# Step columns and differential values in one product, the B by C products of both groups side by side, cumulated sums of both token halves at once

## What is computed

```python
for l in range(DEPTH):                       # DEPTH = 2
    h = rms_norm(x, attn_norm_w[l])
    proj = h @ w_in[l]
    a_q, a_k, a_v, b_z, b_xbc, b_dt, c_q, c_k, c_v = jnp.split(proj, offsets, axis=-1)
    y_a = windowed_gqa_sink(...)             # 6 heads, a_q, a_k, a_v
    y_b = ssd_mixer(b_z, b_xbc, b_dt, ...)   # Mamba-2, both directions, 2 state groups
    y_c = diff_attention(...)                # 4 heads, c_q, c_k, c_v
    x = x + jnp.concatenate([y_a, y_b, y_c], axis=-1) @ w_out[l]
    h = rms_norm(x, ffn_norm_w[l])
    x = x + hierarchical_moe(h, ...)
return rms_norm(x, final_norm_w)
```

## Time and profile before

| | us |
|---|---|
| three runs, median | 1211.71 |
| lowest, highest | 1211.57, 1214.07 |
| span of the profiled execution | 1213.5 |
| its own time, beyond the span | not listed apart |
| TensorE busy | 948.9 (78%) |
| VectorE busy | 398.7 (33%) |
| ScalarE busy | 189.6 (16%) |
| DMA engines, queue 1 | 86.5% of the span |

### The profile page before, as it was taken

One profiled execution on the slowest core, in us unless ns is written; L12 is line 12 of the kernel. 1 busy time (PEld: TensorE's weight loads), 2 busy tenths in 40 slices (PEclk: granted clock), 3 DMA queues, 4 the chain that ended last, 5 costly groups with the idle time before them and its releaser, 6 DMA issues.

```text
span 1213.5 us, 26544 instructions
## 1 busy us (share of the span) xinstructions
PE 948.9 (78%) x11004; PEld 600.0 (49%) x11004; DVE 398.7 (33%) x1231; ACT 189.6 (16%) x546; POOL 8.9 (1%) x27
## 2 busy tenths in 40 slices
PE   7999989766668787895799999895666666666964
PEld 6877855433334443453387777553333333333532
DVE  4778453111122222231176774431111111111213
ACT  2245221000001110110023352110000000000101
POOL 2000000000000000000000000000000000000000
PEclk9999989888789998997899999898888888787977
DMA  9835179999999999999995244899999999999994
GB/s 342 334 123 209 70 296 425 424 427 427 426 424 424 426 426 425 400 425 428 408 394 199 97 182 156 344 426 426 425 428 426 426 427 427 425 425 426 424 423 196
DMA packets 47435, 436.64 MB, mean 360 GB/s; under 512 B 8256, under 2 KB 10304, under 8 KB 21440
## 3 DMA queue, kind: packets, MB, share of 16 engines
q1 hardware_dynamic: 47296, 434.72, 86.5%
HBM read 433.65 MB, written 1.05 MB: 358 GB/s over the span
## 4 chain that ended last, share of the span: by engine, by line
PE 47%; DMA 37%; DVE 6%; issue 5%; SPq 2%; DVEq 2%; ACT 1%; another core or an unknown queue 1%; ACTq 0%
DMA ring<-in_w_up 37%; PE ps L601 13%; PE ps L689 8%; PE ps L617 5%; PE ps L812 4%; PE ps L626 3%; PE ps L569 3%; PE ps L701 2%; PE ps L589 2%; PE ps L706 1%; PE ps L752 1%; SPq L442 1%; SPq L440 1%; PE ps L791 1%
## 5 line engine op out<-in xcount | busy, mean ns | idle before, releaser
L601 PE MATMUL ps<-ring,xg 128*32 128x256 f32 x4352 | 317.3, 455 | 176.9 <-DMA ring<-in_w_up 171.5
L601 PEld LDWEIGHTS ps<-ring,xg 128*32 128x32 f32 x4352 | 170.0, 130 | 307.3 <-issue 247.1
L1135 DVE SCALAR_TENSOR_TENSOR th<-th,ps 128x128 f32<-128x128 f32 x72 | 20.7, 288 | 593.8 <-ACT th L934 593.8
L617 PE MATMUL ps<-ring,actT 128*32 128x256 f32 x2304 | 139.2, 382 | 13.5 <-issue 12.8
L617 PEld LDWEIGHTS ps<-ring,actT 128*32 128x32 f32 x2304 | 69.0, 109 | 74.6 <-DVE actT L1139 22.3
L934 ACT ACTIVATE th<-ps 128x128 f32<-128x128 f32 x72 | 20.0, 278 | 515.7 <-PE ps L601 480.1
L569 PE MATMUL ps<-xh,Pb 128*32 128x256 f32 x1152 | 79.4, 394 | 24.5 <-issue 20.4
L689 PE MATMUL ps<-hT,ring 128*128 128x256 f32 x416 | 95.3, 386 | 0.8 <-ACT hT L971 0.8
L689 PEld LDWEIGHTS ps<-hT,ring 128*128 128x128 f32 x416 | 78.6, 193 | 12.7 <-issue 1.4
L626 PE MATMUL ps<-ysb,PwT 32*128 32x256 f32 x992 | 71.8, 403 | 0.0
L569 PEld LDWEIGHTS ps<-xh,Pb 128*32 128x32 f32 x1152 | 38.5, 113 | 49.3 <-issue 24.5
(11 more groups left out here) (251 smaller groups left out, 744.0 us busy)
## 6 DMA issues: line engine op xcount, KB each, us to landing
ring<-in_w_down SPq DMA_DIRECT2D x62, 2048.0 KB, 40.4
ring<-in_w_gate SPq DMA_DIRECT2D x60, 2048.0 KB, 45.6
ring<-in_w_up SPq DMA_DIRECT2D x60, 2048.0 KB, 47.3
ring<-in_w_in SPq DMA_DIRECT2D x6, 2048.0 KB, 19.8
ring<-in_w_out SPq DMA_DIRECT2D x4, 2048.0 KB, 19.5
ring<-in_w_gate SPq DMA_DIRECT2D x8, 1024.0 KB, 29.1
ring<-in_w_up SPq DMA_DIRECT2D x8, 1024.0 KB, 31.8
ring<-in_w_in SPq DMA_DIRECT2D x4, 1024.0 KB, 21.3
```

The source lines that it names most:

```text
L601: last = mm(b_gate[j * SLOTS:(j + 1) * SLOTS, 0:2 * GQ], tokens[:, k, :], ring[:, low:high + 1:high - low, o:o + GQ], start=(k == 0), stop ...
L617: last = mm(b_y[j * SLOTS:(j + 1) * SLOTS, 0:DQ], actT[:, c * SLOTS:(c + 1) * SLOTS], ring[:, slot, o:o + DQ], start=(c == 0), stop=(c == ...
```

## The change

**The pieces of `w_in`.** The second piece held the last 128 columns of `xbc`, `dt` and `cq`; now it holds those 128, `dt` and `cv`, in two transfers. The fifth piece held `ck` and `cv`; now `cq` and `ck`. The widths stay 396 and 512.

**`dt` and `cv` in one product.** The TensorE steps `dt` and `cv` become `dc.0` and `dc.1`, one per token half, eight products of 268 columns each, at the place where `dt` was. ScalarE copies both into `dcv`, scaled; VectorE's `dt` step reads `dcv` and so waits for ScalarE.

**`cb` on TensorE** becomes one step `cB` where `cb.0` was: four products that alternate between the two 64-row halves, into two banks. ScalarE's `cb.g` copies stay where they were.

**`cum`**: three products over both token halves instead of six.

```diff
-W_IN_PIECES = [(O_XBC, 512), (O_XBC + 512, O_CK - O_XBC - 512), (O_AQ, O_AV), (O_AV, O_XBC - O_AV), (O_CK, D_IN - O_CK)]
+W_IN_PIECES = [[(O_XBC, 512)], [(O_XBC + 512, O_CQ - O_XBC - 512), (O_CV, D_IN - O_CV)], [(O_AQ, O_AV)], [(O_AV, O_XBC - O_AV)],
+               [(O_CQ, O_CV - O_CQ)]]
+DC = 2 * S_H + C_H * C_V
...
-    dt conv.4 ak silu.3 aq.0 dta xs.0 silu.4 sc.0 nm.0 aq.2 xs.1 aS.0 cum cumT aq.1 lam cb.0 sc.1 sc.2 seg.0.0
+    dc.0 dc.1 dt conv.4 ak silu.3 aq.0 dta xs.0 silu.4 sc.0 nm.0 aq.2 xs.1 aS.0 cum cumT aq.1 lam cB cb.0 sc.1 sc.2 seg.0.0
...
-    pT.2 cq.1 sc.5 pT.3 y.5 sc.6 cS.0 sc.7 oa.0 nm.5 ybn pT.4 nm.6 cv oa.1 pT.5 yT.0 yT.1 oa.2 sc.8 sc.9 sc.10
+    pT.2 cq.1 sc.5 pT.3 y.5 sc.6 cS.0 sc.7 oa.0 nm.5 ybn pT.4 nm.6 oa.1 pT.5 yT.0 yT.1 oa.2 sc.8 sc.9 sc.10
     nm.7 pT.6 cS.1 sc.11 sc.12 outA.0 pT.7 outA.1 od.0 nm.8 sc.13 nm.9 pT.8 od.1 outA.2 pT.9 od.2 od.3 outA.3 ycn
...
-    return {"xbc": int(step[-1] == 4), "dt": 1, "cq": 1, "aq": 2, "ak": 2, "vz": 3, "ck": 4, "cv": 4}.get(kind)
+    return {"xbc": int(step[-1] == 4), "dc": 1, "aq": 2, "ak": 2, "vz": 3, "cq": 4, "ck": 4}.get(kind)
...
+                    for c0, w in W_IN_PIECES[n][1:]:
+                        sp_.dma_start(to[:, :, IN_WIDTH[n] - w:], w_in[li, :, c0:c0 + w].rearrange("(k p) n -> p k n", p=P)
+                                      ).then_inc(signal, 16)
...
+                    elif kind == "dc":
                         w = piece(piece_of(s), s)
+                        t = s[1]
+                        for k in range(KC):
+                            last = mm(bank[:, 0:DC], hT[:, k, t * P:(t + 1) * P], w[:, k, P:P + DC], start=(k == 0), stop=(k == KC - 1))
...
+                        sums = bank[:, 0:TT * 4 * S_H].rearrange("p (t n) -> p t n", t=TT)
+                        mm(sums[:, :, 0:S_H], upto[:, :], dta[:, :, 0:S_H], start=True, stop=True)
+                        mm(sums[:, :, S_H:2 * S_H], since[:, :], dta[:, :, S_H:2 * S_H], start=True, stop=True)
+                        last = mm(sums[:, :, 2 * S_H:4 * S_H], ones[:, :], dta[:, :, 0:2 * S_H], start=True, stop=True)
...
+                        for t in range(TT):
+                            for g in range(S_G):
+                                r = slice(g * S_N, (g + 1) * S_N)
+                                last = mm(ps[BANK["cb", g]][:, t * SEQ:(t + 1) * SEQ], xc[r, 3, t * P:(t + 1) * P], xc[r, 4, :],
+                                          start=True, stop=True)
...
+                    elif kind == "dc":
                         act.wait_ge(done["dve"], nth(li, "dve", ("sq",)))
+                        last = A(dcv[:, s[1], :], bank[:, 0:DC], ACT.Copy, scale=root[:, TT + s[1]:TT + s[1] + 1])
...
+                        dve.wait_ge(done["act"], nth(li, "act", ("dc", 0), ("dc", 1)))
+                        v.tensor_tensor(z.rearrange("p (t n) -> p t n", t=TT), dcv[:, :, 0:n],
+                                        rowp[:, R_DTB:R_DTB + n].unsqueeze(1).broadcast_to([P, TT, n]), ALU.add)
```

More of the change, by code:

```diff
@@ L45 @@
 A_SCALE, C_SCALE = A_D ** -0.5, C_QK ** -0.5
-W_IN_PIECES = [(O_XBC, 512), (O_XBC + 512, O_CK - O_XBC - 512), (O_AQ, O_AV), (O_AV, O_XBC - O_AV), (O_CK, D_IN - O_CK)]
+W_IN_PIECES = [[(O_XBC, 512)], [(O_XBC + 512, O_CQ - O_XBC - 512), (O_CV, D_IN - O_CV)], [(O_AQ, O_AV)], [(O_AV, O_XBC - O_AV)],
+               [(O_CQ, O_CV - O_CQ)]]
+IN_WIDTH = [sum(w for _, w in piece) for piece in W_IN_PIECES]
+DC = 2 * S_H + C_H * C_V
 W_OUT_PIECES = [(0, 512), (512, 512)]
@@ L107 @@
 STEPS = [(name, *map(int, index)) for name, *index in (step.split(".") for step in ORDER.split())]
-ON_PE = {"xT", "rs", "xbc", "dt", "cq", "aq", "ak", "cum", "xs", "cb", "cumT", "rows", "aS", "cS", "y", "vz", "pT", "ck", "cv", "oa", "od",
+ON_PE = {"xT", "rs", "xbc", "dc", "cq", "aq", "ak", "cum", "xs", "cB", "cumT", "rows", "aS", "cS", "y", "vz", "pT", "ck", "oa", "od",
          "yT", "cT", "outA", "outB", "fT", "lg", "seed", "cnt", "rank", "ov"}
@@ L111 @@
           "lg", "route", "rank", "ov"}
-ON_ACT = {"sq", "rs", "par", "lam", "dta", "cumT", "silu", "row", "sc", "vz", "zs", "pT", "cv", "oa", "od", "yT", "cT",
+ON_ACT = {"sq", "rs", "par", "lam", "dta", "cumT", "silu", "row", "sc", "vz", "zs", "pT", "dc", "oa", "od", "yT", "cT",
           "xT", "xs", "cb", "sa", "xn2", "route"}
@@ L186, in reader @@
         return "act" if step[1] % 2 == 0 else "dve"
-    return "dve" if step[0] in ("xbc", "cq", "aq", "ak", "ck", "dt", "cum", "sc", "y", "lg", "cnt", "rank", "ov") else "act"
+    return "dve" if step[0] in ("xbc", "cq", "aq", "ak", "ck", "cum", "sc", "y", "lg", "cnt", "rank", "ov") else "act"
 PE_STEPS = list(COUNT["pe"])
@@ L203, in tenants @@
         return [("sc", A_H + 4 * step[1] + i) for i in range(4)]
+    if step[0] == "cB":
+        return [("cb", g) for g in range(S_G)]
     if step[0] == "rows":
@@ L701, in _ @@
                             last = mm(bank[:, :], hT[:, k, t * P:(t + 1) * P], w[:, k, :], start=(k == 0), stop=(k == KC - 1))
-                    elif kind == "cv":
-                        w = piece(piece_of(s), s)
-                        for t in range(TT):
-                            for k in range(KC):
-                                last = mm(bank[:, t * C_H * C_V:(t + 1) * C_H * C_V], hT[:, k, t * P:(t + 1) * P],
-                                          w[:, k, O_CV - O_CK:D_IN - O_CK], start=(k == 0), stop=(k == KC - 1))
                     elif kind == "cum":
@@ L992, in _ @@
                     elif kind == "cb":
+                        act.wait_ge(done["pe"], nth(li, "pe", ("cB",)))
                         last = A(CBs[s[1]][:, :, :].rearrange("p a b -> p (a b)"), bank[:, :], ACT.Copy)
```

46 lines of the change are left out of this document (13 added, 33 removed).

## The result

| | before | after |
|---|---|---|
| median of four runs, side by side | 1212.89 (1211.57 to 1215.15) | 1253.28 (1251.64 to 1254.08) |
| ratio, 95% interval | | 1.0329 (1.0309 to 1.0349) |
| span of the profiled execution | 1213.5 | 1250.8 (its own time 1252.65) |
| mixer of layer 0 (to the first gather of the experts) | 168.72 | 181.44 |
| experts of layer 0 | 438.18 | 446.67 |

The change made the kernel 3.3% slower. The stages are taken from the one profiled execution of each kernel and cut where TensorE's first gather (line 569, after the change 577) starts in each layer and where the last quarter of the experts' result is copied. The span grew by 37.3 us: 12.7 and 16.3 in the two mixers, 8.5 in the experts of layer 0.

A forecast was written before the change was run, and what follows sets the result against it. Experts wait for weights by DMA, the mixer for TensorE, with VectorE pacing its tail. Per layer 2.1 + 8.8 + 3.4 = 14.3 us, twice 28.6, on span 1213.5 gives 1242.1, less 1.8: 1240.3 us; range 1231 to 1252.

The forecast's parts named there:

- The sign: Whole kernel: slower, chance 0.93; faster 0.04, within 0.2% 0.03.
- Part 1: TensorE up to `cq.1`: `dc` +3.9, `cum` −0.7, `cB` −1.1, together +2.1 us per layer (bounds 2.0 to 3.3).
- `cB` paired: `cB` step: four products side by side cost 1.06 us, saving 1.06; if they did not pair, nothing.
- the rule of the Trainium skill weighed there: `dc`: weight loads overlap products only where row groups differ, giving 11.0 us; the forecast took 7.4 instead.
- Part 2: Tail without `cv`: VectorE's chain stays, TensorE idles from about 105.6 to 111.4; 7.17 us removed bring about 1.
- Part 3: Tail: `outA.0` waits for ScalarE's `pT.6` copy, +5.1 us; `outA.1` for VectorE's `sc.12` read, +8.8 per layer in all.
- Part 4: Both `outA` steps: the new waits lower the granted clock, 1.7 us each, +3.4 per layer.
- My reading of the earlier trace: `outB` before the change: two short waits around 143 us lowered the clock, 8.88 us for 7.17, 1.7 lost.
- 14.3 us in each layer: Each layer's mixer: 2.1 + 8.8 + 3.4 us, twice 28.6.
- their restart moves with the end of the mixer: Ring full before the experts: DMA bytes left stay the same, so every microsecond of a mixer's tail counts once per layer.
- the experts' stages as long as before: Experts of both layers: expected sign that the change leaves their length as it was.
- the median 1.8 us under the span: Whole kernel: median of runs 1211.71 against the profiled span 1213.5, so 1242.1 became 1240.3 us.

The follow-up runs named there:

- e1_banks: The changed kernel with PSUM banks renamed from `dc.0` to the first `outA` step, so neither `outA` step waits late for a bank; 1226.29 us, ratio 1.0105.
- e2_waits_alone: The kernel before with only bank numbers changed, so that `pT.6` lies in bank 0 and `sc.12` in bank 1; 1238.39 us, ratio 1.0202.
- the fourteen kernels: The kernels before and after the change and all follow-up kernels; experts of layer 1 took 433.7 to 437.3 us over them.
- the last four: The kernel before with 6, 12, 25 or 38 empty products per layer in the wait for the router's choice; 1218.00, 1221.52, 1236.60, 1239.79 us, one run each.
- e7_cum_cB: The kernel before with only the `cum` and `cB` edits, banks without late waits, no empty products added; 1214.20 us, ratio 1.0019.
- e9_shift38: The kernel before with 38 empty products of 4 columns per layer in the wait for the router's choice; 1239.79 us, one run.

## Why the prediction was wrong

The sign and most of the cause were right; the time was 13.0 us too low and 1.3 us above my range.

*Part 1, +2.1 up to `cq.1`:* `cqT` was copied at 98.65 against 96.92, +1.7: right in kind, 0.4 us too large. `dc` took 7.23 to 7.39 us (7.4 expected) and `cB` paired. By the rule of the Trainium skill weighed there (TensorE: Matmul & The Clock Gate, section Part 3: Packing small matmuls — row/col tiling) `dc` would have taken an estimated 11.0 us; the trace does not follow that rule, and the weight loads of these full-height products stayed hidden.

*Part 2, the lost cover:* a wait of 5.69 us for the gated norm where I had read off 5.8. Right; that the transposes, `oa.2` and `pT.6` behind it run at half speed (1.51 and 1.98 us for 0.84 and 1.09) was not in my sum. In the changed kernel it lies under `outA.0`'s wait; in e1_banks, with that wait gone, it stands on the path.

*Part 3, the banks:* `outA.0` at 123.14, expected 123.3; `outA.1` at 134.96, expected 134.7 with the clock's 1.7 in it. Shown from both sides by e1_banks and e2_waits_alone.

*Part 4, +3.4 for the clock:* the two steps lost 2.2 and 1.7 us in layer 0, 3.9 in all. In layer 1 they took 7.45 and 8.43 us, about 2.1 and 3.2 over full speed, 5.3 in all, so the term was too small there. On the other side `outB` of layer 0 took 7.2 us and not the 8.88 of the earlier trace rows, which gave 1.7 back; in layer 1 it took 8.86. My reading of the earlier trace rows, that two short waits had cost that clock, does not stand: the same two waits (1.18 and 0.69 us) are there after the change, and in layer 0 the clock is 1.00 behind them. Mixers together: 29.0 us, expected 28.6. That the sum fits so well is partly luck: I expected 14.3 us in each layer, and the layers took 12.7 and 16.3.

*The step that failed* is the sentence that the bytes left for the DMA engines are the same "and their restart moves with the end of the mixer", and with it "the experts' stages as long as before": it put the experts at nothing. Layer 1's experts were as long as before (436.29 for 436.43), layer 0's took 8.5 us more, because TensorE's stalls there grew from 13.6 to 23.6 us with 19 products per layer fewer ahead of them. I had read one windows row over 438 us, 0.99 busy, as a pure DMA bound, and had not asked what 19 instructions fewer do to a program with code out of line.

The other part of the gap is how I set the sum against the runs: I took the median 1.8 us under the span, as it stood in the kernel before; after the change it is 2.5 above. In every later run the device time is 1.7 to 1.9 us more than the span of the same execution. So the profiled execution before, with a span of 1213.5, took about 1215.3 us, some 3.6 above the median of the three runs, and I set the span of a long execution against their median. The gap is then made up as follows: 8.5 (experts of layer 0) + 0.4 (mixers) + 4.3 (median against span) = 13.2 us, less 0.2 in what is left of the span.

## What to carry to other kernels

When a table of buffers or banks is worked out from the order, compare it before and after any edit at the places where a fixed buffer is taken: removing a step at one place put waits of 4.6 and 3.8 us at another, and renaming the banks took 25 us of the mixers back. Work that fills a wait costs nothing until it is moved; with the bank waits gone, `cv` taken out of its wait and paid for in the solid run still left the mixers 0.7 and 2.8 us longer than before, not shorter (1.7 us that `outB` of layer 0 lost to the clock before and not here are in the 0.7). A stage that is bound by transfers on average may have a stretch where an engine has to keep up; look at it slice by slice before calling it covered.

## What the runs showed that I had not expected

Removing instructions can cost time far away. TensorE stalls, most of them of 6.4 to 7.5 us, stand ahead of the first gather of some passes that are jumped to; shorter ones, 2.4 to 3.9 us, stand inside such a gather or ahead of later products. How many there are and how long depends on the number of instructions ahead: 13.2 to 27.2 us in layer 0 over the fourteen kernels. What the sequencer waits for there no view shows; that it goes with the position is shown by adding empty products alone. The Trainium skill has a rule that would explain it (Runtime: NRT & Kernel Launch, section Instruction fetch mechanics): instructions are fetched in blocks, ahead and in sequence, and a taken branch to a block that isn't there has to wait for it. The runs agree with it as far as they go, since only position was changed in the last four; no row shows a fetch, so that this is the cause is not shown.

The granted clock drops without idleness too: 0.81 over 9 us in a solid run (e7_cum_cB), and from 1.00 to 0.50 in a stretch without a gap, in the middle of products of 4 columns back to back (e9_shift38). And one profiled execution can be off by such a stretch, 1.7 us in e7_cum_cB.
